# Four output-gate tiles in three passes, low parts made on GpSimd, and another order of taps, inversion, z and gate tiles in the second block's mixer

## The reference, cut to what matters

```python
proj = h @ w_in       # a_qkv, a_z, a_gates, b_qk, b_v, b_o, b_gates, merge
a_qkv = silu(centred_conv(a_qkv, gdn_conv_w))          # 5 taps, 12 tiles of 128 channels
b_qk  = silu(centred_conv(b_qk, mlstm_conv_w))         # 5 taps, 8 tiles
o_a = gated_delta(aq, ak, av, g, beta), both directions, chunks of 64   # needs an inverse per chunk
o_a = rmsnorm(o_a) * silu(a_z)
h_b = mlstm(bq, bk, bv, i_pre, f_pre), both directions
h_b = layernorm(h_b) * sigmoid(b_o)
gate_a, gate_b = split(sigmoid(merge))
y = gate_a * (o_a @ w_branch_a) + gate_b * (h_b @ w_branch_b)
out = y @ w_out
```

## Time and profile before

| | |
|---|---|
| median of 3 runs | 2684.06 us (2683.41 to 2684.5) |
| the profiled execution's own time | 2682.79 us |
| its span in the trace | 2681.0 us |
| PE, PEld busy | 97%, 80% of the span |
| DVE, ACT, POOL busy | 61%, 37%, 2% |
| the second mixer up to the mLSTM's output | about 2058 to 2346 us of the span |

### The profile page before, as it was taken

The page is one execution under the profiler, slowest core; times in us unless marked ns, Lnnn a source line. Parts: engine busy times, 40 slices in busy tenths (PEclk is TensorE's granted clock), DMA queues, the critical chain, the costliest instruction groups (busy, mean ns, idle before and its releaser), DMA issues.

```text
span 2681.0 us, 37410 instructions
## 1 busy us (share of the span) xinstructions
PE 2600.6 (97%) x15326; PEld 2148.8 (80%) x15326; DVE 1634.2 (61%) x2906; ACT 1002.4 (37%) x1777; POOL 66.9 (2%) x91
## 2 busy tenths in 40 slices
PE   8999999999999999999999999998999999999896
PEld 5888888867889888888888898798999787886453
DVE  4867766366446877648767465765555777675221
ACT  5322233266434322234222243664444442543121
POOL 0000000000000000000000000000000000000320
PEclk9999999999999999999999999999999999999998
DMA  7535442200222445434467433134345202149997
GB/s 320 198 155 225 179 182 95 95 32 32 77 112 95 175 178 220 165 126 157 174 250 281 158 123 132 43 134 181 139 180 192 95 32 95 64 172 418 412 395 322
DMA packets 48841, 456.55 MB, mean 170 GB/s; under 512 B 10784, under 2 KB 11168, under 8 KB 13344
## 3 DMA queue, kind: packets, MB, share of 16 engines
q1 hardware_dynamic: 41472, 446.01, 42.9%
q0 software_dynamic: 6912, 6.32, 0.7%
q10 hardware_dynamic: 288, 1.84, 0.2%
HBM read 497.11 MB, written 1.05 MB: 186 GB/s over the span
## 4 chain that ended last, share of the span: by engine, by line
PE 86%; DVE 7%; ACT 3%; DMA 3%; issue 2%; SPq 0%; POOL 0%; ACTq 0%; DVEq 0%; POOLq 0%
PE ps L545 68%; PE ps L3917 2%; PE ps L2038 2%; PE ps L1427 1%; PE ps L1450 1%; DMA BIG<-edn 1%; PE ps L554 1%; DMA BIG<-eup,extra_ids 1%; PE ps L3943 1%; PE nb L3943 1%; ACT fh L532 1%; DMA wr<-ws 1%; PE ps L3957 1%; PE ps L2664 1%; DVE fl L539 1%
## 5 line engine op out<-in xcount | busy, mean ns | idle before, releaser
L539 DVE TENSOR_TENSOR fl<-wr,fh 128x1024 fp32r<-128x1024 f32 (+2 forms) x436 | 481.9, 1107 | 446.0 <-ACT fh L532 445.2
L545 PE MATMUL ps<-UL,fh 128*128 128x512 f32 (+1 forms) x2096 | 731.9, 349 | 11.5 <-DVE UL L894 5.3
L545 PE MATMUL ps<-UH,fl 128*128 128x512 f32 (+1 forms) x2096 | 729.5, 348 | 0.0
L545 PE MATMUL ps<-UH,fh 128*128 128x512 f32 (+1 forms) x2096 | 729.1, 348 | 0.0
L532 ACT CAST fh<-wr 128x1024 fp32r<-128x1024 f32 (+2 forms) x436 | 414.4, 954 | 321.0 <-PE ps L545 298.8
L545 PEld LDWEIGHTS ps<-UL,fh 128*128 128x128 f32 x2096 | 397.7, 190 | 65.5 <-DVE UL L894 6.0
L545 PEld LDWEIGHTS ps<-UH,fh 128*128 128x128 f32 x2096 | 397.9, 190 | 49.8
L545 PEld LDWEIGHTS ps<-UH,fl 128*128 128x128 f32 x2096 | 397.7, 190 | 49.5
L597 DVE SCALAR_TENSOR_TENSOR acc<-wr,CA 128x1024 f32<-128x1024 f32 x256 | 312.4, 1220 | 3.7
L545 PE MATMUL ps<-HL,fh 128*128 128x512 f32 (+1 forms) x770 | 267.4, 347 | 0.0
L545 PE MATMUL ps<-HH,fl 128*128 128x512 f32 (+1 forms) x770 | 266.9, 347 | 0.0
(11 more groups left out here) (624 smaller groups left out, 3833.2 us busy)
## 6 DMA issues: line engine op xcount, KB each, us to landing
wr<-ws SPq DMA_DIRECT2D x135, 2048.0 KB, 8.1
wr<-ws SPq DMA_DIRECT2D x32, 1408.0 KB, 6.1
wr<-eup SPq DMA_DIRECT2D x27, 1024.0 KB, 17.3
BIG<-eup SPq DMA_DIRECT2D x26, 1024.0 KB, 14.2
wr<-edn SPq DMA_DIRECT2D x12, 1024.0 KB, 11.2
wr<-ws SPq DMA_DIRECT2D x11, 1024.0 KB, 6.9
BIG<-edn SPq DMA_DIRECT2D x11, 1024.0 KB, 10.0
X<-eup SPq DMA_DIRECT2D x6, 1024.0 KB, 11.6
```

What stands on the lines that cost most here:

```text
L539: e.tensor_tensor(lv, raw_tile(sp.units[n]), hv.bitcast(F32), ALU.subtract).then_inc(*low_done.inc("low", event))
L545: i = e.matmul(out, l, r, start=first and n == 0, stop=last and n == len(pairs) - 1, skip_group_check=True)
```

## The change

Cut to its core; moved lines with their places.

```diff
 late_free(n), n < 4:
-                return [("cross product", 7)]
+                return [("o gate", n, "used")]

+        def act_o_high(e, q):
+            u = o_units[q]
+            e.wait_ge(*at("loaded", late_load(u)))
+            e.wait_ge(*at("cross product", 7))
+            e.copy(late_parts(u)[0], late_tile(weights(late_load(u)), u)).then_inc(*hi_done.inc("high", u))
+
+        def pool_lows(e):
+            for u in o_units + late_units[0:4]:
+                h, l = late_parts(u)
+                e.wait_ge(*at("high", u))
+                e.tensor_tensor(l, late_tile(weights(late_load(u)), u), h.bitcast(F32), ALU.subtract).then_inc(*pool_low.inc("low", u))

 def act_conv(e, tag, n):
-            e.copy(xp[:, 2:258], psum.of("conv in", tag, n)[:, 0:256]).then_inc(*act.inc("conv in", tag, n))
+            n, load, q, wn, dst = conv_tiles(tag)[n]
+            b = psum.of("conv in", tag, n)
+            e.copy(xp[:, 2:258], b[:, 0:256]).then_inc(*act.inc())
+            e.activation(dst, b[:, 0:256], ACT.Identity, scale=col("cva" if tag == "gdn" else "cvb", wn * 5 + 2, 1)).then_inc(
+                *act.inc("conv in", tag, n))

 def dve_conv(e, tag, n):
-            e.tensor_scalar(dst, xp[:, 0:256], col(ck, wn * 5, 1), None, ALU.mult).then_inc(*dve.inc())
-            for i in range(1, 5):
...
+            for i in (0, 1, 3, 4):
...

 def dve_solve(e):
             for n in range(2):
+                dve_rhs(e, 2 + n)
                 for _ in dve_conv(e, "mlstm", n):

 def pe_o_gate(e, q):
-            pe_tile(e, "o gate", q, ("win2", 3616, 512), q, q == 3)
+            pe_late_tile(e, "o gate", q)

 def act_proj_b(e):
+            act_o_high(e, 0)
             for tt in range(2):
...
-                act_late_high(e, tt)
+                act_o_high(e, 1 + tt)
+            act_o_high(e, 3)
             for q in range(4):
                 act_o_gate(e, q)
-                if q % 2:
-                    act_late_high(e, 2 + q // 2)
+                act_late_high(e, q)

 def dve_proj_b(e):
-            for n in range(2):
-                dve_late_low(e, n)
-                yield

 pe_second:
-                if 1 <= h <= 4:
-                    pe_tile(e, "z", h - 1, ("win2", 1536, 512), h - 1, h == 4)
+                if h % 2:
+                    pe_tile(e, "z", h // 2, ("win2", 1536, 512), h // 2, h == 7)

 dve_second:
-                for _ in range((0, 0, 0, 0, 1, 1, 1, 2)[h]):
+                for _ in range((0, 0, 0, 0, 1, 1, 1, 1)[h]):
...
-                for _ in range(2 if n < 14 else 5):
+                for _ in range(2 if n < 5 or 7 <= n < 11 else 4 if n < 7 else 7):
                     next(invert, None)

 dve_beside:
-            for h in range(4):
+            for h in range(2):
                 dve_rhs(e, h)

 pe_gdn_out (act_gdn_out alike):
             pe_gate_b(e, 0)
+            pe_gate_b(e, 1)
...
-                pe_gate_b(e, f + 1)
+                pe_gate_b(e, f + 2)

 dve_gdn_out:
-            dve_late_low(e, 2)
...
-                dve_late_low(e, 3 + f)
+                if f:
+                    dve_late_low(e, 3 + f)
+                if f == 1:
+                    dve_end_blocks(e, "mlstm", MP[:, 20:24])

 pe_mlstm (act_mlstm alike):
-                if h in (1, 3, 5):
-                    pe_gate_b(e, 5 + h // 2)
+                if h in (1, 3):
+                    pe_gate_b(e, 6 + h // 2)

 dve_mlstm:
-            dve_end_blocks(e, "mlstm", MP[:, 20:24])

 gpsimd block:
             pool_second(e)
+            pool_lows(e)
             pool_expert_loads(e)
```

More of the change, by code:

```diff
@@ L380, in program @@
         router_in = tally("router_in")
+        pool_low = tally("pool_low_parts")
         ident_in = tally("ident_in")
@@ L1936, in program @@
                      for i, o in enumerate([cross_at + 1024 * x for x in range(4)] + [uv_at + 1024, inv_at, inv_at + 1024, 1024])]
+        o_units = [("o gate", q) for q in range(4)]
         late_units = [("gate b", j) for j in range(8)] + [("gate a", 0), ("branch pair", 0)] \
@@ L1941, in late_load @@
             tag, j = u
+            if tag == "o gate":
+                return "win2", 3616, 512
             return ("br2", 0) if tag == "branch pair" else ("win2", (GATE_B if tag == "gate b" else GATE_A) + 512 * (j // 4), 512)
@@ L1950, in late_parts @@
         def late_parts(u):
-            n = late_units.index(u)
+            n = u[1] if u[0] == "o gate" else late_units.index(u)
             h = late_sets[n % 4 if n < 8 else 4 + n % 4][:, :]
@@ L2064, in dve_conv @@
             e.wait_ge(*at("conv in", tag, n))
-            e.tensor_scalar(dst, xp[:, 0:256], col(ck, wn * 5, 1), None, ALU.mult).then_inc(*dve.inc())
-            for i in range(1, 5):
-                before = dve.now()
-                yield
-                e.wait_ge(*before)
+            for i in (0, 1, 3, 4):
+                if i:
+                    before = dve.now()
+                    yield
+                    e.wait_ge(*before)
                 e.scalar_tensor_tensor(out=dst, in0=xp[:, i:i + 256], scalar=col(ck, wn * 5 + i, 1), in1=dst,
@@ L2713, in pe_late_tile @@
                 e.wait_ge(*at(*old))
-            if u == late_units[0]:
+            if u == o_units[0]:
                 e.wait_ge(*at("late u", 3))
@@ L2929, in act_second, with act_z @@
                     act_conv(e, "gdn", 10 + (h - 2) // 3)
+            def act_z(q):
+                e.wait_ge(*at("z proj", q))
+                e.copy(z_raw[:, q, :], psum.of("z", q)[:, 0:256]).then_inc(*act.inc("z", q))
             for h in range(8):
@@ L2933, in act_second @@
                     act_to_tokens(e, "v a", vtok)
-                if 2 <= h <= 5:
-                    e.wait_ge(*at("z proj", h - 2))
-                    e.copy(z_raw[:, h - 2, :], psum.of("z", h - 2)[:, 0:256]).then_inc(*act.inc("z", h - 2))
+                if h in (2, 4, 6):
+                    act_z(h // 2 - 1)
                 if h == 3:
@@ L2940, in act_second @@
                     act_log_exp(e)
+            act_z(3)
             e.wait_ge(*at("products sum", 7))
@@ L3067, in act_gdn_out @@
             act_gate_b(e, 0)
+            act_gate_b(e, 1)
             for f in range(4):
@@ L3223, in act_mlstm @@
                 act.mark("exp decay", "mlstm", h)
-                if h in (1, 3, 5):
-                    act_gate_b(e, 5 + h // 2)
+                if h in (1, 3):
+                    act_gate_b(e, 6 + h // 2)
                 if h % 2:
```

3 lines of the change are left out of this document (1 added, 2 removed).

## The result

The changed kernel takes **2690.61 us** (median of 11 runs, 2687.53 to 2698.38) where the kernel before takes 2683.41 (11 runs, 2682.09 to 2687.23): a ratio of 1.0029, 95% interval 1.0021 to 1.0036. It is slower by 7.2 us, more than the 0.2% that counted as no change; the range holds it, the sum does not. The profiled execution spans 2688.8 us where that of before spans 2681.0. In what follows, times of stages come from one profiled execution of each kernel.

A forecast was written before the change was run, and what follows sets the result against it. PE, busy 97% of the span, was taken as the bound. Terms 0.3 - 4.9 + 8.6 + 2.4 - 4.0 = +2.4 us on the 2684.06 us median gave 2686.5 us, range 2674 to 2694.

The forecast's parts named there:

- the likeliest case: Whole kernel: the prediction's own sum, 2686.5 us for the median, called "same"; chance 0.43.
- Taps: Conv stage: scaled copies move from DVE to ACT, hidden except where PE waits for ACT's squares; +0.3 us (0 to +0.7).
- z tiles, inversion, right-hand sides: Heads and start of solve: DVE's idle gaps filled, 3.0 us gained plus 1.9 of low clock; -4.9 us (-8 to 0).
- Scan stage: POOL's subtractions lock out DVE, 1.0 + 10.0 us, less 2.4 for two low parts leaving DVE; +8.6 us.
- GDN out: PE waits 1.2 us for DVE's low part of gate b in two of four turns; +2.4 us (0 to +3).
- mLSTM: Ends ready early, -1.9, and two thirds of one gate b tile leaving the heads, -2.1; -4.0 us (-5 to -1).
- Keeps its low clock: mLSTM stage: the first gate b tile, 4.95 us, was said to stay at low clock.
- The 2.0 us a wait: Scan stage: DVE's loss per large POOL subtraction, scaled by elements from a 0.25 us wait; bounds 0.25 and 3.5.
- POOL barely holds DVE: Scan stage: long subtractions hardly delay DVE, stage -0.9, sum -7.1, 2677.0 us; chance 0.33.
- POOL is slower than I take it: Scan stage: subtractions take 3.5 us each, stage +17.6, sum +11.4, 2695.5 us; chance 0.16.
- The chunks give nothing: Heads before the solve: PE's bank waits replace the old wait, the -4.9 falls away, 2691.4 us; chance 0.08.
- The clock: Scan stage: more PE idle could lower its clock, lengthening o gate tiles behind DVE's waits; given no term and no chance.

The follow-up runs named there:

- e5: The changed kernel with four shares of work drawn beside each solve step in `dve_solve` instead of five: 2688.03 us, ratio 1.0015 to the kernel before.
- e8: e7 with every conv tap on VectorE again and five shares drawn per solve step: 2672.88 us, ratio 0.9964 to the kernel before.
- e3: The changed kernel with each of POOL's eight subtractions replaced by a memset, which reads nothing: 2684.25 us, ratio 0.9995 to the kernel before.
- e3b: The changed kernel with each of POOL's eight subtractions replaced by a copy, which reads one operand: 2681.64 us, ratio 0.9997 to the kernel before.
- e4: The changed kernel with each of POOL's eight 128x1024 subtractions cut into eight of 128x128: 2687.12 us, ratio 1.0012 to the kernel before.
- e6: The changed kernel with VectorE's low parts of gate b 4 to 7 made one head earlier in GDN out: 2687.37 us, ratio 1.0012 to the kernel before.
- e7: The changed kernel with the edits of e5 and e6, o gate in one f32 pass, POOL making only gate b 0 and 1 low parts: 2672.55 us, ratio 0.9961.
- e1: The kernel before with only the change's first half (conv taps, z tiles, inversion shares, right-hand sides): 2684.68 us, ratio 1.0004 to the kernel before.

## Why the prediction was right or wrong

The range held the result, the likeliest case did not: 2686.5 was said and "same" by a measure of 0.2%, 2690.6 came, 0.29% over before. By its steps:

- **Taps, +0.3: too small.** The wait for the squares grew by 0.36 us (0.70 to 1.06), as said. A second one of 0.43 us at 2121.24, for ACT's longer conv step, had no term. Together 0.8, of which 0.7 is left at head 0.
- **z tiles, inversion, right-hand sides, -4.9: right here, and short of one term.** The solve is reached 3.25 us sooner after head 0, its first records are at full clock, about 1.6 us more, which is the term. What the prediction missed is that a conv tile with one step less breaks the count of five in `dve_solve`: +2.0 us, shown by e5 and again by e8. It put the two right-hand sides into "time DVE now has free" and did not ask what the drawing of five then reaches. The low clock of 2134 to 2146 stayed, at 0.57.
- **Scan stage, +8.6: right, +9.3.** The length (2.2 said, 2.35 measured), the lock for the whole instruction, and the count of one short and five long waits: 11.0 said, 11.2 measured. e3, e3b and e4 show the cause, not only the size. The part that the estimate took as reading time is what is left of the whole instruction, up to 2.1 us a wait; more on this below. As said, the marker came 34 us after DVE's first state product (2282.46 - 2248.06), and PE waited inside the stage, 5.58, and at its end.
- **GDN out, +2.4: right, +3.0.** Two waits of 1.35 for the low part, 1.2 said; e6 takes them away. The rest is ACT's norm at head 0, 7.35 us behind the `o` product for 7.07.
- **mLSTM, -4.0: right in the sum, -5.0, with another working.** The wait for the ends is gone. "Keeps its low clock" was wrong: the first gate b tile takes 4.30 us for 4.95, as the low stretch is shorter. The whole of the tile that left counts, 3.1, not two thirds. This stage turns on the clock: with the new order of gate tiles it takes 40.3 us at full clock (e6, e7) and 42.4 to 43.9 with a low stretch (the others); with the old order it is 47.4 before and 48.9 in e1. What brings the stretch is not shown.

The 2.0 us a wait came near by luck. The row that was scaled, a DVE product at 630.78 that took 0.25 us too long, stood beside POOL's next subtraction, which the earlier trace rows does not show:

```profile
630.26 0.90 POOL L1728 TENSOR_TENSOR CA<-rot 128x127 f32<-128x127 f32 x1
```

It ends at 631.16, 0.38 us after the DVE product began. The 0.25 is what was left of it, less 0.13, and no reading time that grows with the elements. The product at 2257.32 began 2.11 us before POOL's end and lost 1.96, which is 0.15 less.

The rivals: *POOL barely holds DVE* falls, by DVE's rows and by e3. *POOL is slower than I take it*: 2.35 us, under the 2.6 from which it was to decide; not this. *The chunks give nothing* was wrong in its place, as the heads do gain, but e1 shows that alone they gain nothing by the end; in its profile a longer low stretch takes most of it. *The clock* had no term for the scan stage, and that was nearly right: the clock did fall to 0.50 behind PE's wait, and 0.42 us of it reached DVE. In the mLSTM stage it is worth 2 to 3.6 us between the profiles here, which the bounds there, -5 to -1, did not name. So the sum's failure, +2.4 for +7.2 us between the medians, 4.8, is 2.0 of solve, 0.4 of taps, 0.7 and 0.6 of two stages held a little small, less 1.0 in the mLSTM, and some 2 us of parts that the change does not touch, which stay unsettled.

## What to carry to other kernels

Before a free engine is given work, ask not only how long it takes there but what it locks: GpSimd's subtractions were never late themselves and made VectorE 11.2 us longer and the stage 9.3, and two of them in VectorE's idle time cost nothing that shows. Where an order is made by drawing a fixed number of steps per round, a change in the number of steps moves waits in a place the change does not name; recount it. And a stage that falls to the low clock in one execution and not in another hides a saving of 2 to 3 us: compare its clock before a gain or a loss there is put down to an edit.

## What was new about the hardware

A writing GpSimd instruction does not hold VectorE's two-operand products, but it held a multiply with one operand. In e3, beside two memsets (2257.03, 1.90 us):

```profile
2258.02 1.05 DVE L2808 TENSOR_SCALAR BIG<-BIG 64x256 f32<-64x256 f32 x1
2259.10 1.69 DVE L2262 TENSOR_TENSOR_SCAN BIG<-BIG 32x64 f32<-32x64 f32 x8
...
2264.95 1.41 DVE L2609 TENSOR_TENSOR acc<-BIG,CA 64x512 f32<-64x512 f32 x2
```

The multiply takes 0.28 alone and ends 0.14 us after the second memset; the pair of L2609, with another memset beside it (2265.32, 0.96 us), keeps its 1.41. So of my third theory for e3 (writes lock by their length) one part stands. The Trainium skill, SBUF — State Buffer, section "Who interferes with whom", has both: a GpSimd instruction that only writes leaves VectorE's two-input instructions alone, while copies and `tensor_scalar` can run in a mode that takes both port pairs and then contend with any. The traces agree for the memset, for `tensor_scalar` (1.05 us for 0.28) and for the lock by whole instructions that e4 shows. The DVE copies that met a POOL instruction in the scan stage were all of 32x1, and none was held: 0.14 us at 2270.18 in e3 beside the memset at 2269.85, and the same at 2268.31 in e3b beside the copy at 2268.16.

A GpSimd subtraction of 1024 elements a partition took 2.35 us, a copy 1.04, a memset 0.95, and one of 128 elements 0.45 us beside the scans (eight in 3.34 us while VectorE was idle). From copy to subtraction, one more operand and an operation, the time more than doubles; which of the two costs it no run parts.
